# Five phase borders worked off in two halves of the tokens

## The chip, the cores and the metric

The kernel runs on one core of a Trainium2 chip. The metric is the device time of one execution in microseconds (us), as the median of the timed runs. TensorE does the matmuls (its weight loads are recorded apart), VectorE and ScalarE the elementwise work, GpSimd splits the weights, and SyncE issues the large transfers.

## The reference, cut to what matters

512 tokens of 1024 features go through three transformer layers: one with an HGRN2 and stick-breaking mixer, one with an mLSTM mixer (both with a gated feed-forward of 2816 features behind a short convolution), and one with dilated and sparse attention and a gated feed-forward. Each layer twice does the same around its mixer or feed-forward:

```python
h = rmsnorm(x, g) * (1.0 + scale) + shift     # scale, shift, gate: from c, one value per feature
x = x + gate * (inner(h) @ w_out)             # the next norm needs all 1024 features of x
```

Between the second and the third layer `x` is normed once more with `final_g`, so that border needs two means in a row. All is float32.

## The kernel before, in words

Activations lie transposed: 8 tiles of 128 features by 512 tokens (`X`). Every float32 product is three fp32r matmuls over high and low parts (`three`, L442): weights high by data high, weights high by data low, weights low by data high. Each has 128 x 128 weights and 512 moving columns, and loads its weights anew.

The weights come as one stream of 302 chunks of 128 x 1024. SyncE loads them into two raw slots, GpSimd splits each into `w_hi` and `w_lo` (`split_at`, L417) in one of four slots (`SPL`), and TensorE raises `pe_done` after each chunk. GpSimd may split chunk n once `pe_done` shows chunk n-4 used, and it first does a one-column operation (`pool_gate`).

The borders are these: even_out to ffn0, down0 to odd_in, odd_out to ffn1, down1 to idx_in (the one with two means), attn_out to ffn2. Called 1 to 5 below. An out phase has 8 chunks, one for each output tile (`tile_chunk`, 24 matmuls); a down phase has 24 chunks, three for each output tile (8, 8 and 6 blocks, 66 matmuls). Output tiles land in the PSUM banks `G[0..3]` in turn.

At a border the engines do this. VectorE adds the gated output tile to `X` (`residual`, L1032), ScalarE squares the tile into one of two slots (`square`, L1636), VectorE adds the square to `sq_acc` (L1299), for the last tile not. TensorE sums `sq_acc` and the last square over the features with one-column float32 matmuls (`norm_scale`, L536), with some idle-filling matmuls (`keep_warm`) between. ScalarE takes the root, VectorE the reciprocal, TensorE spreads it over the partitions (`bcast`, L558). Then, for each of 8 tiles: VectorE multiplies by gain and row factor (`scaled`, L1087, one input from PSUM) into one of four `work` slots, ScalarE adds the shift and rounds to `h_hi` (L1651), VectorE takes the rest as `h_lo` (`low`, L1091, from `work` and `h_hi`, both in SBUF). `scaled` runs two tiles ahead of `low`. TensorE starts the next phase with `first_tiles` (L475), which goes through the 8 tiles once and does each for two chunks, so that it uses a tile as soon as it is there. The order on each engine is written out by hand; each engine works its queue in order and waits on counting semaphores.

Of the kernel before, what the change touches and what calls it, by code (L numbers as in the profile page):

```python
# [26 lines left out]
F32 = mybir.dt.float32  # L27
# [6 lines left out]
P = 128  # L34
# [42 lines left out]
WARM = (2, 4, 4, 14)  # L77

# [88 lines left out]
def build(nc, x_in, wstream, adastream, c_in, cols_in, const_in, mask_in, gatew_in, wiw_in, wuk_in, wuv_in, out):  # L167
    with ExitStack() as ctx:
# [155 lines left out]
        rstd_bc = sem("rstd_bcast")  # L324
        t_ready = sem("t_tiles")
# [115 lines left out]
        def _(pe):  # L441
            def three(out_ap, w_h, w_l, r_h, r_l, first, last):  # L442
                pe.matmul(out_ap, w_h, r_h, start=first, stop=False)  # L443
                pe.matmul(out_ap, w_h, r_l, start=False, stop=False)  # L444
                return pe.matmul(out_ap, w_l, r_h, start=False, stop=last)  # L445
# [46 lines left out]
            def tiles(phase, bodies, done=0, wide=2):  # L492
                if done == 0 and phase in FILL:

                    first_tiles(phase, FILL[phase], wide)
# [10 lines left out]
            def down(phase, p_fill):  # L506
                with pe.Fori(0, 2) as i:
                    c = 0
                    for m in range(4):
                        k = 0  # L510
                        pe.wait_ge(gfree[m], i + G0[phase][m])
                        for nk in DOWN:
                            pe.wait_ge(w_split, 12 * i + N0[phase] + c + 1)
                            for kk in range(nk):
                                if m == 0:
                                    pe.wait_ge(p_ready, FT * p_fill + k + 1)
                                s = (N0[phase] + c) % SPL
                                mm = three(G[m][:], whi[s][:, kk * P:(kk + 1) * P], wlo[s][:, kk * P:(kk + 1) * P],
                                           Phi[:, k, :], Plo[:, k, :], k == 0, k == FT - 1)
                                k += 1  # L520
                            mm.then_inc(pe_done, 1)
                            c += 1
# [6 lines left out]
            def partial_sums(c0, tile, first, last):  # L529

                for j in range(NTB):
# [3 lines left out]

            def norm_scale(r):  # L536

                pe.wait_ge(sq_added, KT * r + KT - 1)
                partial_sums(0, sqacc, True, False)
# [3 lines left out]
                if r == 4:  # L543
                    pe.wait_ge(gsq_added, KT)
                    partial_sums(4, work[:, 2, :], False, False)
                    pe.wait_ge(gsq_ready, KT)
                    mm = partial_sums(4, work[:, 1, :], False, True)
                mm.then_inc(norm_sum, 1)
                keep_warm(3 if r == 4 else 1)
# [14 lines left out]
            def norm(r):  # L564
                norm_scale(r)
                bc[0] += 1
                bcast(rstdps, bc[0])
                if r not in (0, 6):
                    keep_warm(WARM[2])

# [178 lines left out]
            tiles("even_out", 2)  # L749
            norm(1)  # L750
            tiles("ffn0", 11)
            down("down0", 0)
            norm(2)

            tiles("odd_in", 2)
# [108 lines left out]
            for u in range(4):  # L864
                tile_chunk(4 + N0["odd_out"] + u, (N0["odd_out"] + u) % SPL, u, 1 + G0["odd_out"][u])
            norm(3)
            tiles("ffn1", 11)
            down("down1", 1)

            norm_scale(4)  # L870
            bc[0] += 1
            bcast(rstdps, bc[0] + 1, 8)
            keep_warm(WARM[2])

            first_tiles("idx_in", FILL["idx_in"])

            bc[0] += 1
# [124 lines left out]
            tiles("attn_out", 2)  # L1002
            norm(5)
            tiles("ffn2", 11)
            down("down2", 2)
# [4 lines left out]
        def _(dve):  # L1010
# [36 lines left out]

            def inverse_rms(n, src):
# [16 lines left out]
            def norm(r, fill, g, shift_scale, first_gain=None):  # L1065

                rms_n[0] += 1
                a = acol[:, 8 * r:8 * r + 8]
# [3 lines left out]
                if first_gain is None:  # L1072
                    ready(inverse_rms(4, rms_n[0]))
                else:
                    ready(inverse_rms(4, rms_n[0]))
                    dve.wait_ge(rstd_ready, inverses_done[0])

                    rms_n[0] += 1
                    link(dve.tensor_tensor(a, a, first_gain, ALU.mult))
                    link(dve.tensor_tensor(rst[:, 4:8], rst[:, 0:4], rst[:, 0:4], ALU.mult))  # L1080
                    dve.tensor_tensor(rst[:, 4:8], rst[:, 4:8], normps[:, 4:8], ALU.mult).then_inc(sig("second_mean"), 1)
                    dve.wait_ge(rms_ready, rms_n[0])
                    link(dve.reciprocal(rst[:, 8:12], rms[:, 8:12]))
                    ready(dve.tensor_tensor(rst[:, 8:12], rst[:, 8:12], rst[:, 0:4], ALU.mult))
                spread()

                def scaled(k):  # L1087
                    dve.scalar_tensor_tensor(out=work[:, k % 4, :], in0=X[:, k, :], scalar=a[:, k:k + 1], in1=rstdps[:],
                                             op0=ALU.mult, op1=ALU.mult).then_inc(t_ready, 1)

                def low(k):  # L1091

                    dve.wait_ge(hhi_ready, KT * fill + k + 1)
                    b = shift_scale[0] + k
                    dve.scalar_tensor_tensor(out=Hlo[:, k, :], in0=work[:, k % 4, :], scalar=modv[:, b:b + 1],
                                             in1=Hhi[:, k, :].bitcast(F32), op0=ALU.add, op1=ALU.subtract).then_inc(h_ready, 1)
# [194 lines left out]
            def residual_tiles(phase, r, gate):  # L1291

                dve.wait_ge(mod_added, gate // 4 - 1)
                for m in range(KT):
                    residual(N0[phase] + m, m, m % 4, gate)
                    if m < KT - 1:
                        add_square_prev(r, m)

            def add_square_prev(r, m):  # L1299
                dve.wait_ge(sq_ready, KT * r + m + 1)  # L1300
                dve.wait_ge(sq_added, KT * r + m)
# [8 lines left out]
            norm(1, 2, col("norm_ffn_g", 0, 8), (24, 32))  # L1310
# [31 lines left out]
            def down(phase, r, gate, group=None, turn=0, gain=False):  # L1342
# [4 lines left out]
                for i in range(2):  # L1347
                    for m in range(4):
                        residual(12 * i + N0[phase] + 3 * m + 2, 4 * i + m, m, gate)
# [12 lines left out]
            norm(2, 3, col("norm_mix_g", 8, 8), (48, 56))  # L1362
# [138 lines left out]
            norm(3, 5, col("norm_ffn_g", 8, 8), (72, 80))  # L1501
            ffn("ffn1", 1, COL["fconv_w"] + 66, 25, 21, C2, 11)
            down("down1", 4, 88, gain=True)
            norm(7, 6, col("g_attn", 0, 8), (96, 104), first_gain=col("final_g", 0, 8))
# [119 lines left out]
            norm(6, 8, col("g_ffn", 0, 8), (120, 128))  # L1624
# [6 lines left out]
        def _(act):  # L1631
            link = Link(act, act_step)
            nrm = [0]
            scaled = [0]

# [3 lines left out]
            def norm(r, fill, shift, table=None):  # L1639
                nrm[0] += 1  # L1640
                act.wait_ge(norm_sum, nrm[0])
                act.activation(rms[:, 0:4], normps[:, 0:4], ACT.Sqrt, bias=col("eps"), scale=1.0 / D).then_inc(rms_ready, 1)
                if table is not None:
                    act.preload_act_table(table)
                high_tiles(shift)

            def high_tiles(shift):
                for k in range(KT):

                    act.wait_ge(t_ready, scaled[0] + k + 1)  # L1650
                    act.activation(Hhi[:, k, :], work[:, k % 4, :], ACT.Identity, bias=modv[:, shift + k:shift + k + 1]).then_inc(hhi_ready, 1)  # L1651
                scaled[0] += KT

# [153 lines left out]
            def squares(r, phase, gain=None):  # L1807

                act.preload_act_table(ACT.Sqrt)
                with act.Fori(0, 2) as i:  # L1810
                    for u in range(4):

                        act.wait_ge(gfree[u], i + G0[phase][u] + 1)
                        act.wait_ge(sq_added, 4 * i + KT * r + u - 1)
                        square(4 * i + u, u % 2)
                        if gain is not None:
                            act.wait_ge(gsq_added, 4 * i + u + 1)
                            act.activation(work[:, u % 2, :], X[:, ds(4 * i + u, 1), :].rearrange("p a t -> p (a t)"), ACT.Square,
                                           scale=cols[:, ds(4 * i + gain + u, 1)]).then_inc(gsq_ready, 1)

            squares(1, "even_out")
            norm(1, 2, 24, ACT.Gelu_apprx_tanh)
# [23 lines left out]

            act.wait_ge(pe_done, N0["odd_in"])
# [3 lines left out]
            norm(2, 3, 48, ACT.Silu)  # L1851
# [77 lines left out]
            norm(3, 5, 72, ACT.Gelu_apprx_tanh)  # L1929
# [198 lines left out]
```

## Time and profile before

| | us |
|---|---|
| median of 3 timed runs (lowest, highest) | 2023.68 (2023.48, 2025.96) |
| profiled execution, whole | 2021.82 |
| profiled execution, span from first to last instruction | 2020.0 |
| TensorE busy | 1947.8 (96%) |
| GpSimd busy | 1183.6 (59%) |
| VectorE busy | 1048.7 (52%) |
| ScalarE busy | 447.2 (22%) |

Times within the execution are counted from its first instruction. A busy engine is one with an instruction on record; a matmul's record is longer than the step from one matmul to the next, since they are pipelined. float32 matmuls (not fp32r) leave two records each. The mean granted TensorE clock was 0.983 of full.

### The profile page before, as it was taken

The page shows a single profiled execution, that of the slowest core. Times are in us where ns is not written, and L with a number is a line of the kernel's source. Part 1 is how long each engine was busy: PE and PEld are TensorE (multiplying, and loading weights), DVE is VectorE, ACT ScalarE, POOL GpSimd, SP SyncE. Part 2 cuts the span into 40 slices and gives each one's busy share as a digit, 9 for nine tenths or more (in the row PEclk, how much of TensorE's full clock was granted, in tenths as well). Part 3 has the DMA queues.
Part 4 walks back from the last instruction along what each step waited for, and adds up shares of the span by engine and source line. Part 5 has one row for each costly group of instructions (what it writes and reads, how often), then busy time and mean ns, then how long its engine had stood idle before and what let it go on. Part 6 is the DMA issues. An engine that isn't in the chain of part 4 may idle for free.

```text
span 2020.0 us, 25249 instructions
## 1 busy us (share of the span) xinstructions
PE 1947.8 (96%) x8772; PEld 1563.7 (77%) x8772; DVE 1048.7 (52%) x1588; ACT 447.2 (22%) x762; POOL 1183.6 (59%) x907
## 2 busy tenths in 40 slices
PE   7999999999999999998999999999997899999998
PEld 6787868888888877655888888886775588888886
DVE  5566257766646353557666663234857563232222
ACT  3302342112110022432221111012116421111100
POOL 3653325878877956223688787743550157666673
PEclk7999999999999999998999999999999999999999
DMA  7432223555555422111355553321210023232232
GB/s 298 167 125 73 94 94 104 188 187 203 188 200 179 156 91 83 42 42 46 133 201 193 194 188 127 104 95 63 84 63 22 11 84 104 93 101 97 95 113 73
DMA packets 67518, 242.25 MB, mean 120 GB/s; under 512 B 7642, under 2 KB 8026, under 8 KB 67458
## 3 DMA queue, kind: packets, MB, share of 16 engines
q1 hardware_dynamic: 65536, 237.01, 34.2%
q10 hardware_dynamic: 1922, 4.40, 0.6%
q8 instruction: 42, 0.69, 0.1%
q14 instruction: 18, 0.15, 0.0%
HBM read 239.28 MB, written 2.10 MB: 119 GB/s over the span
## 4 chain that ended last, share of the span: by engine, by line
PE 89%; DVE 4%; ACT 3%; issue 2%; DMA 1%; POOL 1%; SPq 0%; DVEq 0%; ACTq 0%; POOLq 0%
PE gemm L443 24%; PE gemm L445 23%; PE gemm L444 23%; PE gemm L470 2%; PE gemm L472 2%; PE gemm L471 2%; DMA w_raw<-wstream 1%; PE mix L646 1%; PE mix L443 1%; PE gemm L799 1%; PE mix L444 1%; PE mix L445 1%; PE mix L952 1%; PE gemm L813 1%; PE mix L554 1%
## 5 line engine op out<-in xcount | busy, mean ns | idle before, releaser
L427 POOL TENSOR_TENSOR w_lo<-w_raw,w_hi 128x1024 fp32r<-128x1024 f32 x302 | 741.1, 2454 | 25.2
L443 PE MATMUL gemm<-h_hi,w_hi 128*128 128x512 f32 x1616 | 635.4, 393 | 14.3 <-DVE h_lo L1123 6.4
L444 PE MATMUL gemm<-h_lo,w_hi 128*128 128x512 f32 x1616 | 631.1, 391 | 0.0
L445 PE MATMUL gemm<-h_hi,w_lo 128*128 128x512 f32 x1616 | 631.0, 390 | 0.0
L424 POOL TENSOR_TENSOR pool_gate<-pool_gate 128x1 f32<-128x1 f32 x298 | 104.2, 350 | 764.6 <-PE gemm L445 619.7
L443 PEld LDWEIGHTS gemm<-h_hi,w_hi 128*128 128x128 f32 x1616 | 305.0, 189 | 83.9 <-issue 13.4
L425 POOL TENSOR_SCALAR w_hi<-w_raw 128x1024 fp32r<-128x1024 f32 x302 | 351.1, 1163 | 18.4 <-DMA w_raw<-wstream 18.4
L445 PEld LDWEIGHTS gemm<-h_hi,w_lo 128*128 128x128 f32 x1616 | 304.7, 189 | 64.0
L444 PEld LDWEIGHTS gemm<-h_lo,w_hi 128*128 128x128 f32 x1616 | 305.2, 189 | 62.7
L1017 DVE CUSTOM_DVE_ANT_0 ada_raw<-ada_raw,c_act 128x1024 f32<-128x1024 f32 x128 | 219.4, 1730 | 106.2 <-DMA ada_raw<-adastream 106.2
L445 PE MATMUL gemm<-p_hi,w_lo 128*128 128x512 f32 x528 | 205.4, 389 | 0.0
L443 PE MATMUL gemm<-p_hi,w_hi 128*128 128x512 f32 x528 | 205.4, 389 | 0.0
L444 PE MATMUL gemm<-p_lo,w_hi 128*128 128x512 f32 x528 | 205.4, 389 | 0.0
L1035 DVE SCALAR_TENSOR_TENSOR x_res<-gemm,modv,x_res 128x512 f32<-128x512 f32 x48 | 35.9, 749 | 245.6 <-PE gemm L445 245.6
L1330 DVE TENSOR_TENSOR work<-work,gemm 128x512 f32<-128x512 f32 x66 | 45.4, 688 | 176.4 <-PE gemm L445 138.6
L1637 ACT ACTIVATE sq_tile<-x_res 128x512 f32 (+1 forms) x56 | 35.3, 631 | 448.5 <-DVE x_res L1035 435.4
L1332 DVE TENSOR_TENSOR p_lo<-work,p_hi 128x512 f32 x66 | 95.0, 1440 | 61.4 <-ACT p_hi L1842 61.4
L1302 DVE TENSOR_TENSOR sq_acc<-sq_acc,sq_tile 128x512 f32<-128x512 f32 x42 | 95.8, 2282 | 37.1 <-ACT sq_tile L1637 37.1
L443 PEld LDWEIGHTS gemm<-p_hi,w_hi 128*128 128x128 f32 x528 | 99.1, 188 | 20.7
L445 PEld LDWEIGHTS gemm<-p_hi,w_lo 128*128 128x128 f32 x528 | 99.1, 188 | 20.5
L444 PEld LDWEIGHTS gemm<-p_lo,w_hi 128*128 128x128 f32 x528 | 99.1, 188 | 20.5
L1836 ACT ACTIVATE work<-work 128x512 f32<-128x512 f32 x44 | 27.8, 633 | 308.8 <-DVE work L1325 308.8
(323 smaller groups left out, 1999.9 us busy)
## 6 DMA issues: line engine op xcount, KB each, us to landing
w_raw<-wstream SPq DMA_DIRECT2D x302, 512.0 KB, 3.5
ada_raw<-adastream SPq DMA_DIRECT2D x128, 512.0 KB, 4.3
a_early<-adastream SPq DMA_DIRECT2D x8, 1024.0 KB, 13.2
out<-x_res SPq DMA_DIRECT2D x8, 256.0 KB, 2.2
x_res<-x_in SPq DMA_DIRECT2D x2, 512.0 KB, 6.4
c_act<-c_in ACTq DMA_DIRECT2D x2, 512.0 KB, 7.2
x_res<-x_in ACTq DMA_DIRECT2D x2, 512.0 KB, 9.0
b_dist<-const_in ACTq DMA_DIRECT2D x1, 512.0 KB
```

The costliest lines, as they stand in the source:

```text
L424: pool.tensor_tensor(pgate[:], pgate[:], pgate[:], ALU.mult)
L425: pool.tensor_scalar(whi[s][:], raw[:, u % RAW, :], 1.0, 0.0, ALU.mult, ALU.add).then_inc(w_hi_done, 1)
L427: pool.tensor_tensor(wlo[s][:], raw[:, u % RAW, :], whi[s][:].bitcast(F32), ALU.subtract).then_inc(w_split, 1)
L443: pe.matmul(out_ap, w_h, r_h, start=first, stop=False)
L444: pe.matmul(out_ap, w_h, r_l, start=False, stop=False)
L445: return pe.matmul(out_ap, w_l, r_h, start=False, stop=last)
L470: pe.matmul(G[j][:], a, wh, start=(k == 0), stop=False)
L471: pe.matmul(G[j][:], a, wl, start=False, stop=False)
L1017: dve.tensor_tensor_reduce(w, w, c, 1.0, start, ALU.mult, ALU.add, total).then_inc(ada_used, 1)
L1302: dve.tensor_tensor(sqacc[:], sqacc[:], sqt[:, m % 2, :], ALU.add).then_inc(sq_added, 1)
L1330: dve.tensor_tensor(work[:, 2 + jj, :], y, G[2 * jj + 1][:], ALU.mult).then_inc(gfree[2 * jj + 1], 1)
L1332: dve.tensor_tensor(Plo[:, ds(2 * i + jj, 1), :].rearrange("p a t -> p (a t)"), work[:, 2 + jj, :], Phi[:, ds(2 * i + jj, 1), :].rearrange ...
```

## The change

At each of the five borders, the last output tile is computed for tokens 0 to 255 first and for tokens 256 to 511 after, the first half into `G[3]`, the second into `M[1]`, with the same weights loaded again. The sums, roots, row factors, `scaled`, `h_hi` and `h_lo` are done for each half on its own, with 256 columns; the sums and row factors of the first half stand among TensorE's matmuls of the second half of the last tile (`BACK` says before which block), and those of the second half among the first-half matmuls of the next phase's first two chunks (`FRONT`). The next phase's first two chunks are done for all 8 tiles of the first half and then for all 8 of the second. `PLACES` says behind which `low` VectorE puts the second half's residual and reciprocal, and where ScalarE puts square, root and the load of the next function table. The chunk counter `pe_done` of the last output tile rises in its second half only.

At odd borders the square of tile 6 is no longer added to `sq_acc` by VectorE but summed by TensorE (`ADDS`). The `keep_warm` matmuls at the five borders are gone. ScalarE's small loads for odd_in and idx_in are issued after the last `h_hi`, not before the norm. The `Fori` loops of the down phases and of `squares` are unrolled.

```diff
+HALVES = (slice(0, 256), slice(256, 512))
+ADDS = {1: 6, 2: 7, 3: 6, 4: 7, 5: 6, 6: 7}
+BACK = {1: (0, 1, 3), 2: (0, 1, 5), 3: (0, 1, 3), 4: (0, 1, 9), 5: (0, 1, 3)}
+FRONT = {1: (2, 5), 2: (2, 4), 3: (2, 5), 4: (3, 7), 5: (2, 5)}
+PLACES = {1: (1, 4), 2: (7, 7), 3: (1, 4), 4: (4, 7), 5: (1, 4)}
...
+            def first_halves(phase, r):
+                late, spread = FRONT[r]
...
+                for half, cols in enumerate(HALVES):
+                    for k in range(KT):
+                        if half == 0 and k == late:
+                            last_sums(r, 1)
+                        if half == 0 and k == spread:
+                            half_rows(r, 1)
+                        if half == 0:
+                            pe.wait_ge(h_half, KT * (r - 1) + k + 1)
+                        else:
+                            pe.wait_ge(h_ready, KT * FILL[phase] + k + 1)
+                        for u in range(2):
+                            if half == 0 and k == 0 and u == 0:
+                                pe.wait_ge(w_split, N0[phase] + 2)
+                            s = (N0[phase] + u) % SPL
+                            mm = three(G[u][:, cols], whi[s][:, k * P:(k + 1) * P], wlo[s][:, k * P:(k + 1) * P],
+                                       Hhi[:, k, cols], Hlo[:, k, cols], half == 0 and k == 0, k == KT - 1, True)
+                            if half == 1 and k == KT - 1:
+                                mm.then_inc(pe_done, 1)
+
+            def last_halves(n, counts, hi, lo, uses, r):
+                early, late, spread = BACK[r]
+                pe.wait_ge(gfree[3], uses)
+                for half, cols in enumerate(HALVES):
+                    out_ap = (G[3], M[1])[half][:, cols]
+                    k = 0
+                    for c, nk in enumerate(counts):
+                        s = (n + c) % SPL
+                        if half == 0:
+                            pe.wait_ge(w_split, n + c + 1)
+                        for kk in range(nk):
+                            if half == 1 and k == early:
+                                first_sums(r)
+                            if half == 1 and k == late:
+                                last_sums(r, 0)
+                            if half == 1 and k == spread:
+                                half_rows(r, 0)
+                            mm = three(out_ap, whi[s][:, kk * P:(kk + 1) * P], wlo[s][:, kk * P:(kk + 1) * P],
+                                       hi[:, k, cols], lo[:, k, cols], k == 0, k == sum(counts) - 1)
+                            k += 1
+                        if half == 1:
+                            mm.then_inc(pe_done, 1)
+                    if half == 0:
+                        mm.then_inc(half_done, 1)
...
@@ VectorE, norm
+                after_residual, after_inverse = PLACES[r]
+                residual_half(last, gate, r, 0)
+                inverse(0)
                 scaled(0)
                 scaled(1)
-                for k in range(KT):
-                    low(k)
-                    if k + 2 < KT:
-                        scaled(k + 2)
+                n = 2
+                for t in range(2 * KT):
+                    low(t)
+                    if t == after_residual:
+                        residual_half(last, gate, r, 1)
+                    if t == after_inverse:
+                        inverse(1)
+                    while n < 2 * KT and n <= t + 2 and (n < KT or t >= after_inverse):
+                        scaled(n)
+                        n += 1
...
@@ ScalarE, norm
+                square_half(r, 0, gain)
+                roots_of(r, 0)
+                for t in range(2 * KT):
...
+                    act.activation(Hhi[:, k, cols], work[:, k % 4, cols], ACT.Identity,
+                                   bias=modv[:, shift + k:shift + k + 1]).then_inc(hhi_ready if half else hhi_half, 1)
+                    if t == min(after_residual + 1, after_inverse):
+                        square_half(r, 1, gain)
+                    if t == after_inverse:
+                        roots_of(r, 1)
+                        if table is not None:
+                            act.preload_act_table(table)
```

## Rows read from the trace of the kernel before

**Rows 1.** Page, parts 1 and 4: busy shares; the last chain's share by engine.
```profile
PE 1947.8 (96%) x8772; PEld 1563.7 (77%) x8772; DVE 1048.7 (52%) x1588; ACT 447.2 (22%) x762; POOL 1183.6 (59%) x907
...
PE 89%; DVE 4%; ACT 3%; issue 2%; DMA 1%; POOL 1%; SPq 0%; DVEq 0%; ACTq 0%; POOLq 0%
```
**Rows 2.** Chain of waits at border 1: start us, us, engine and tile.
```profile
337.79 0.79 PE mix L532 x8
...
343.89 0.76 DVE h_lo L1095
...
344.90 0.47 PE gemm L443
```
**Rows 3.** TensorE's timeline at border 4: start us, us, line, operation.
```profile
1339.96 0.95 PE L532 MATMUL mix<-cst,sq_acc 128*128 128x1 f32 x8
...
1351.21 0.47 PE L443 MATMUL gemm<-h_hi,w_hi 128*128 128x512 f32 x1 [0.86 <-DVE h_lo L1095]
```
**Rows 4.** Timeline of all engines at border 1.
```profile
332.86 0.39 PE L443 MATMUL gemm<-h_hi,w_hi 128*128 128x512 f32 x1
332.86 0.19 PEld L444 LDWEIGHTS gemm<-h_lo,w_hi 128*128 128x128 f32 x1
...
337.39 0.40 PE L445 MATMUL gemm<-h_hi,w_lo 128*128 128x512 f32 x1
...
337.63 0.95 PE L532 MATMUL mix<-cst,sq_acc 128*128 128x1 f32 x8
337.83 0.75 DVE L1035 SCALAR_TENSOR_TENSOR x_res<-gemm,modv,x_res 128x512 f32<-128x512 f32 x1 [1.17 <-PE gemm L445]
...
338.09 1.05 POOL L425 TENSOR_SCALAR w_hi<-w_raw 128x1024 fp32r<-128x1024 f32 x1
...
338.50 0.65 DVE L1070 SCALAR_TENSOR_TENSOR acol<-modv,cols 128x8 f32<-128x8 f32 x1
...
339.22 2.35 POOL L427 TENSOR_TENSOR w_lo<-w_raw,w_hi 128x1024 fp32r<-128x1024 f32 x1
...
340.84 1.28 ACT L1644 ACT_TABLE_LOAD   x1
...
342.35 1.41 DVE L1088 SCALAR_TENSOR_TENSOR work<-x_res,acol,mix 128x512 f32<-128x512 f32 x2 [1.25 <-PE mix L554]
```
**Rows 5.** TensorE's timeline: eight transposes in a row.
```profile
1547.61 1.09 PE L971 MATMUL gemm<-cst,ada_raw 128*128 128x128 f32 x8
```
**Rows 6.** Timeline of weight loads: sixteen for one-column matmuls in a row.
```profile
1342.68 1.87 PEld L532 LDWEIGHTS mix<-cst,work 128*128 128x128 f32 x16
```
**Rows 7.** Groups by form (busy us, mean ns | idle); one line's runs (min/median/max ns).
```profile
L1526 DVE SCALAR_TENSOR_TENSOR b_score<-ada_raw,b_wi,b_score 128x256 f32<-128x256 f32 x7 | 3.3, 477 | 0.0
...
L1095 DVE SCALAR_TENSOR_TENSOR h_lo<-work,modv,h_hi x40: 744/746/753, 343.9 to 1656.0; 128x512 fp32r<-128x512 f32 x40
```
**Rows 8.** GpSimd's busy time while ffn0's first two chunks run.
```profile
345.00:355.90 10.90, 0.43 (x2) 1.00 0.07 26
```
**Rows 9.** Timeline of VectorE and GpSimd in the attention stage.
```profile
1474.54 1.23 POOL L425 TENSOR_SCALAR w_hi<-w_raw 128x1024 fp32r<-128x1024 f32 x1
1474.89 4.21 DVE L1567 SCALAR_TENSOR_TENSOR b_bias<-b_dist 128x512 f32<-128x512 f32 x2
1475.85 2.70 POOL L427 TENSOR_TENSOR w_lo<-w_raw,w_hi 128x1024 fp32r<-128x1024 f32 x1
```
**Rows 10.** All runs of two VectorE lines: min/median/max ns, first and last start.
```profile
L1567 DVE SCALAR_TENSOR_TENSOR b_bias<-b_dist x8: 677/684/2874, 1474.9 to 1528.5; 128x512 f32<-128x512 f32 x8
L1302 DVE TENSOR_TENSOR sq_acc<-sq_acc,sq_tile x42: 693/2588/2727, 306.2 to 1994.2; 128x512 f32<-128x512 f32 x42
```
**Rows 11.** Stretches: length, busy PE, PEld, DVE, ACT, POOL, then granted clock.
```profile
1345.00:1347.00 2.00, 2.00 (x7) 1.38 (x6) 1.00 (x6) 0.30 (x1) 0.00 (x0) 0.51 0.95 327
1484.00:1487.00 3.00, 1.01 (x5) 0.50 (x3) 0.00 (x0) 1.96 (x4) 1.83 (x3) 1.00 0.53 173
1487.00:1492.00 5.00, 4.75 (x19) 3.80 (x20) 1.23 (x7) 1.39 (x2) 1.72 (x1) 0.66 0.30 106
```

More of the change, by code:

```diff
@@ L493, in tiles, with out_tiles @@
+            def out_tiles(phase, r):
+                for u in range(3):
+                    tile_chunk(4 + N0[phase] + u, (N0[phase] + u) % SPL, u, 1 + G0[phase][u])
+                last_halves(N0[phase] + 7, (KT,), Hhi, Hlo, 1 + G0[phase][3], r)
+            def tiles(phase, bodies, done=0, wide=2, halves=None):
                 if done == 0 and phase in FILL:
-                    first_tiles(phase, FILL[phase], wide)
+                    if halves:
+                        first_halves(phase, halves)
+                    else:
+                        first_tiles(phase, FILL[phase], wide)
@@ L748, in _ @@
             pe.wait_ge(h_ready, KT * FILL["even_out"] + 7)
[L749 to L755, printed above, removed]
+            tiles("even_out", 1)
+            out_tiles("even_out", 1)
+            tiles("ffn0", 11, halves=1)
+            down("down0", 0, 2)
+            tiles("odd_in", 2, halves=2)
             pe.wait_ge(sig("gw_split"), 1)
@@ L863, in _ @@
                 tile_chunk(N0["odd_out"] + u, (N0["odd_out"] + u) % SPL, u, G0["odd_out"][u])
[L864 to L877, printed above, removed]
+            out_tiles("odd_out", 3)
+            tiles("ffn1", 11, halves=3)
+            down("down1", 1, 4)
+            first_halves("idx_in", 4)
             bcast(M[1], bc[0])
@@ L1001, in _ @@
                 values(p)
[L1002 to L1005, printed above, removed]
+            tiles("attn_out", 1)
+            out_tiles("attn_out", 5)
+            tiles("ffn2", 11, halves=5)
+            down("down2", 2, 6)
             norm(6)
@@ L1063, in _, with norm @@
             rms_n = [0]
[L1065 to L1068 removed]
+            def norm(r, slot, fill, g, shift_scale, last, gate, first_gain=None):
+                a = acol[:, 8 * slot:8 * slot + 8]
                 dve.wait_ge(mod_added, shift_scale[1] // 4 - 1)
@@ L1085, in norm @@
[L1085 to L1093, printed above, removed]
-                    b = shift_scale[0] + k
-                    dve.scalar_tensor_tensor(out=Hlo[:, k, :], in0=work[:, k % 4, :], scalar=modv[:, b:b + 1],
-                                             in1=Hhi[:, k, :].bitcast(F32), op0=ALU.add, op1=ALU.subtract).then_inc(h_ready, 1)
+                    ready(dve.reciprocal(rst[:, c], rms[:, c]))
@@ L1647, in high_tiles, with roots_of @@
[L1647 to L1651, printed above, removed]
-                scaled[0] += KT
+                c = slice(2 * half, 2 * half + 2)
+                act.activation(rms[:, c], normps[:, c], ACT.Sqrt, bias=col("eps"), scale=1.0 / D).then_inc(rms_ready, 1)
+            def roots_of(r, half):
+                root(half)
+                if r == 4:
+                    act.wait_ge(sig("second_mean"), half + 1)
+                    act.activation(rms[:, 8 + 2 * half:10 + 2 * half], rst[:, 4 + 2 * half:6 + 2 * half], ACT.Sqrt, bias=col("eps"),
+                                   scale=1.0 / D).then_inc(rms_ready, 1)
@@ L1809, in squares @@
                 act.preload_act_table(ACT.Sqrt)
[L1810 to L1819, printed above, removed]
+                last_use[0] = G0[phase][3] + 2
+                for m in range(KT if r not in PLACES else KT - 1):
+                    act.wait_ge(gfree[m % 4], m // 4 + G0[phase][m % 4] + 1)
+                    act.wait_ge(sq_added, ADDED[r] + m)
+                    square(m, m % 2)
+                    if gain is not None:
+                        act.wait_ge(gsq_added, m + 1)
+                        act.activation(work[:, m % 2, :], X[:, m, :], ACT.Square, scale=gain[:, m:m + 1]).then_inc(gsq_ready, 1)
             squares(1, "even_out")
-            norm(1, 2, 24, ACT.Gelu_apprx_tanh)
+            norm(1, 24, None, ACT.Gelu_apprx_tanh)
             def ffn(phase, f, taps, bias):
```

217 lines of the change are left out of this document (148 added, 69 removed).

## The prediction

> **What bounds the kernel now.** First I read the page's shares: TensorE is busy 96% of the span and 89% of the chain that ended last runs over it [rows 1]. Other engines count only where TensorE waits. The chain of waits at one border shows such a place: after the last out matmul it goes from the norm's one-column sums through the rest of the norm to the first h_lo, and only then to the first matmul of the next phase [rows 2]. The same chain stands at five borders; the fourth, with a second mean, is longer [rows 3].
>
> The timeline gives the step of a full matmul: 21 of them from 332.86 to 337.39, so 4.53/20 = 0.2265 us [rows 4]. Its record is 0.39 to 0.40 long, so a record outlasts the streaming by 0.163, and the last out matmul streams until 337.63, where the sums begin [rows 4]. The first of the next phase streams from about 344.98 (its record ends at 345.37; 345.37 - 0.163 - 0.2265) [rows 2]. So a normal border costs 7.35 us. The fourth costs 11.33 by the same reckoning, from 1339.96 to 1351.29 [rows 3].
>
> I count each border from the start of its last out chunk to the end of the next phase's first two chunks (48 matmuls, 10.87 us). Before, with 24 matmuls in a last chunk (borders 1, 3, 5): 5.44 + 7.35 + 10.87 = 23.66. With 66 (border 2): 14.95 + 7.35 + 10.87 = 33.17. Border 4: 14.95 + 11.33 + 10.87 = 37.15.
>
> **TensorE's own work after.** Each of those matmuls becomes two of 256 columns: 144 at an odd border, 228 at an even one, 888 in all. No row shows such a matmul. Half of 0.2265 is 0.1133. An instruction pair that loads 128 columns of weights steps by (1.09 - 0.28)/7 = 0.116 in the transposes [rows 5]. If the excess of 0.2265 over 512 columns at 2.4 GHz (0.2133) is a fixed price, the step is 0.1067 + 0.013 = 0.120. I take 0.12; the bounds are 0.113 and, if the load hid nothing, 0.189 + 0.107 = 0.30, from the load's record [rows 4]. That upper end is far from the transposes' 0.116, where load and matmul already overlap. The norm's f32 passes stay and step by about 0.112 (16 loads in 1.87 us: 1.87 less the last one's 0.19, over 15) [rows 6]: 32 passes at odd borders, 24 at border 2, 40 at border 4. The keep-warm matmuls go. So with no wait at all an odd border takes 144 x 0.12 + 32 x 0.112 = 20.9, border 2 30.1, border 4 31.8.
>
> The row on loads: the next load is issued beside the running matmul (start 332.86 for both) and the step stays 0.2265, although load and stream together would be about 0.32 [rows 4]. The Trainium skill, page "TensorE: Matmul & The Clock Gate", section "Part 3: Packing small matmuls", says a weight load overlaps a running matmul only where the row groups differ. By it 888 matmuls would step by some 0.21 instead of 0.12 and the change would lose about 80 us more; this trace, with full-height loads, disagrees.
>
> **VectorE, with nothing in its way.** A border now needs 16 scaled and 16 h_lo operations of 256 columns. The nearest row (same instruction and two SBUF inputs, 256 columns) is 0.477, against h_lo's 0.746 for 512 [rows 7]. Two scaled tiles in a row take 1.41, so they step by 0.66, 0.083 less than the record [rows 4]; half ones then step by 0.394, a half tile costs VectorE 0.79 against TensorE's 0.72. At an odd border (0 is the start of the last chunk): first half ends at 2.88; half residual 3.08 to 3.56; square to 4.0, hidden by the sums over sq_acc; last sums 5.03; root, reciprocal, rows 6.39; scaled 7.03; h_lo 0 at 8.09, ready when TensorE is through the second half at 8.64. That is the gain: the 7.35 is gone. But 16 half tiles from there, plus the second residual and reciprocal and the 1.28 us table load [rows 4], which now sits between h_hi 4 and 5, put h_lo 15 at 21.3 and TensorE's end at 22.7. Gain 1.0 each, VectorE-bound. Border 2: its first half tiles hide beneath 66 matmuls; end 30.6, gain 2.6. Border 4: 33.4, gain 3.8. Sum 3 x 1.0 + 2.6 + 3.8 = 9.4 us faster.
>
> **VectorE beside GpSimd.** This decides my sign. h_lo reads two SBUF tiles (work and h_hi). All its 40 runs took 0.744 to 0.753 [rows 7], but in none of them did GpSimd split: its two operations in the gap end at 341.57 [rows 4], and in the 10.9 us of the first two chunks it is busy 0.43 [rows 8], since all four weight slots are full. Other VectorE instructions of two SBUF inputs did meet GpSimd's splitting. A scalar_tensor_tensor of 0.684 took 2.874 at its longest [rows 10]: two in a row took 4.21, the first held until w_hi ended, the second, which found w_lo just started, until w_lo ended; and that w_lo took 2.70 for 2.40, as it had waited for the first [rows 9]. The eight-column gain at 338.50 ended with w_hi after 0.65 [rows 4], and the squares' adds have a median of 2.588 against a minimum of 0.693 [rows 10]. Residual and scaled, with one input in PSUM, keep 0.75 beside GpSimd [rows 4].
> The Trainium skill, page "SBUF — State Buffer", section "Who interferes with whom", says that a VectorE instruction with two SBUF inputs contends with a GpSimd one that reads SBUF, for the whole instruction. By h_lo's own rows the sum would stay at 9.4 faster; by the rule, which the rows of other lines bear out, it turns.
>
> After the change they meet. A chunk is split as soon as TensorE frees its slot: w_hi begins 0.46 us after the last matmul (337.63 to 338.09), w_lo ends at 341.57, and the next gate follows [rows 4]; some 3.6 us a chunk. At an odd border the last chunk's slot comes free at 8.64, so w_hi and w_lo fall on h_lo 2 and 3: w_lo holds h_lo 3 from 10.75 to 12.82. Some of that hides the table load. End 23.7: gain 0.
> At border 2 the three last chunks (8, 8, 6) are needed by both halves, and their slots come free only in the second, at 12.6, 15.5 and 17.6. GpSimd then splits three chunks in a row, 13.1 to 25, each stretched to 3.95 by two h_lo that slip in between its operations. Only those two get through per chunk: h_lo 7 starts at 25.0 instead of 18.3. The new order puts the second residual behind h_lo 7, and TensorE stands in its queue, before tile 2 of the next phase, at the wait for that half's squares: from 19.1 to 26.5, with tiles 2 to 7 and all later matmuls behind it. Then come the sums, rows and 14 tiles: 26.5 + 0.9 + 14 x 0.72 = 37.4. Loss 4.3. Border 4, residual after h_lo 4: the same meeting gives 38.9, loss 1.75. Sum 3 x 0 + 4.3 + 1.75 = 6.0 us slower.
>
> The clock: it read 1.00 while TensorE worked; in 1345 to 1347, after it had done only one-column sums and short keep-warm work, it read 0.51, and 0.66 after a stretch with 1.0 us of work in 3 [rows 11]. An idle of 7.4 us at border 2 should do the same: some 3.4 us at 1.2 GHz lose 1.7, all on the path; border 4 hides most, 0.5. Sum 8.2.
>
> The rest at nothing. The small loads of odd_in and idx_in are issued after the last h_hi instead of before the norm: 1.3 and 1.8 us on ScalarE's queue, then VectorE's splits; TensorE has two chunks (10.9 us) before it needs a freed bank. If that cover fails, about 2 us. Unrolled loops and static addresses: within 1 us either way.
>
> **Forecast.** The profiled execution took 2021.82 (span 2020.0 and 1.8 around it) and lies 1.9 below the median of the timed runs, 2023.68. 2021.8 + 8.2 = 2030.0; as a median 2031.9.
>
> **Rivals.**
> - Other side, faster: the meetings don't happen or don't hold h_lo. Speaking for it: no h_lo row shows one. Against it: rows of the same instruction form. The modelled nine meetings with a w_lo (one at each odd border, three at each even one) cost 9.4 + 6.0 = 15.4, 1.7 each; the sign turns where five or fewer of them fall on the path. 2023.7 - 9.4 = 2014.3.
> - Milder: they meet, but the third chunk's w_raw is late, its split falls into the gap of sums and root, and the clock stays up. Border 2 then loses about 1.5, border 4 nothing, odd ones gain 0.3: 2024.5.
> - Half matmuls far dearer, 0.19 (the load's record as the step): 888 x 0.07 = 62 more, partly under VectorE's pace: about 2085.
>
> **Chances.** Forecast 0.50 (own range 2026 to 2040: steps of 0.113 to 0.13 give -2.8 to -10.8 before the clock), faster rival 0.24, milder 0.22, dear matmuls 0.04. The range 2014 to 2040 leaves out the last and the edges. 0.2% is 4 us, what this kernel's measurement can tell from no change. Slower: 0.44 + 0.07 + 0.04 = 0.55; same: 0.05 + 0.14 + 0.02 = 0.21; faster 0.24.
>
> **What would show it.** h_lo of 256 columns with a median near 0.48 but a maximum near 2.6, and GpSimd busy beside it at borders 2 and 4. TensorE idle some 7 us before tile 2 of odd_in, waiting for the square. The half matmuls' step: 0.12. Odd borders ending within 1 us of 23.7. Wrong if h_lo's maximum stays below 0.6, or if the split of the held chunks falls elsewhere.

## The result, and the profile after

The changed kernel takes 2037.01 us (median of 4, 2036.82 to 2037.63) against 2023.58 for the kernel before (4 runs, 2023.15 to 2025.96): ratio 1.0067, 95% interval 1.0055 to 1.0080. It is 13.4 us slower, where 8.2 was forecast. The profiled executions differ by 15.2 us of span (2035.2 against 2020.0); the mean granted clock fell from 0.983 to 0.977.

The lengths of the five borders, in us, each from the first matmul of the last out chunk to the end of the next phase's first two chunks (border 4: to the spreading of row factors that stands right behind those two chunks), read from TensorE's timeline. The forecast counted from 23.66, 33.17 and 37.15; the timeline of the kernel before gives 0.04 to 0.08 more:

| border | before | forecast | after |
|---|---|---|---|
| 1 | 23.72 | 23.7 | 24.46 |
| 2 | 33.25 | 39.1 (37.4 and 1.7 of clock) | 39.55 |
| 3 | 23.70 | 23.7 | 24.57 |
| 4 | 37.22 | 39.4 (38.9 and 0.5) | 41.69 |
| 5 | 23.71 | 23.7 | 23.16 |

Their sum is 11.8 us more than before, 6.3 of it at border 2 and 4.5 at border 4. The other 3.4 lie outside the borders: 2.2 before border 1, where the code is unchanged, and 1.1 between borders 4 and 5. More on them below.

The page's parts 1 and 4 answer to [rows 1]: TensorE is as busy as before, and VectorE's share of the last chain is up from 4% to 6%.

```profile
PE 1951.1 (96%) x9166; PEld 1588.3 (78%) x9166; DVE 1077.2 (53%) x1679; ACT 460.7 (23%) x814; POOL 1188.1 (58%) x907
...
PE 87%; DVE 6%; ACT 2%; issue 2%; DMA 1%; POOL 1%; SPq 0%; DVEq 0%; ACTq 0%; POOLq 0%
```

TensorE's timeline after shows the step of half a matmul: 24 of them start between 334.43 and 337.18, 2.75/23 = 0.12 us, the forecast value, against 0.2265 for a whole one [rows 4].

```profile
334.43 0.28 PE L462 MATMUL gemm<-h_hi,w_hi 128*128 128x256 f32 x1
...
337.18 0.28 PE L464 MATMUL gemm<-h_hi,w_lo 128*128 128x256 f32 x1
```

The query of h_lo's line (min/median/max in ns) answers to the last of [rows 7]. The median is what a free half tile takes; the maximum is that of a held one, as in [rows 10]:

```profile
L1217 DVE SCALAR_TENSOR_TENSOR h_lo<-work,modv,h_hi x80: 472/480/2229, 342.3 to 1673.1; 128x256 fp32r<-128x256 f32 x80
```

VectorE's timeline at border 2, and then GpSimd's over the same microseconds. Each h_lo that starts beside a w_hi or a w_lo ends just after it (705.76 + 1.03 = 706.79 on a w_hi that ends at 706.52; 707.11 + 2.23 = 709.34 on a w_lo that ends at 709.06). The scaled tiles, with one input in PSUM, stay at 0.47 in the same stretch. Two h_lo get through per chunk, as forecast (the row of 2.56 holds two, 2.17 and 0.47):

```profile
705.76 1.03 DVE L1217 SCALAR_TENSOR_TENSOR h_lo<-work,modv,h_hi 128x256 fp32r<-128x256 f32 x1
706.72 0.47 DVE L1205 SCALAR_TENSOR_TENSOR work<-x_res,acol,mix 128x256 f32<-128x256 f32 x1
707.11 2.23 DVE L1217 SCALAR_TENSOR_TENSOR h_lo<-work,modv,h_hi 128x256 fp32r<-128x256 f32 x1
...
710.99 2.19 DVE L1217 SCALAR_TENSOR_TENSOR h_lo<-work,modv,h_hi 128x256 fp32r<-128x256 f32 x1
...
714.82 2.56 DVE L1217 SCALAR_TENSOR_TENSOR h_lo<-work,modv,h_hi 128x256 fp32r<-128x256 f32 x2
717.31 0.47 DVE L1156 SCALAR_TENSOR_TENSOR x_res<-mix,modv,x_res 128x256 f32<-128x256 f32 x1
```
```profile
705.47 1.05 POOL L444 TENSOR_SCALAR w_hi<-w_raw 128x1024 fp32r<-128x1024 f32 x1
706.61 2.45 POOL L446 TENSOR_TENSOR w_lo<-w_raw,w_hi 128x1024 fp32r<-128x1024 f32 x1
709.02 0.37 POOL L443 TENSOR_TENSOR pool_gate<-pool_gate 128x1 f32<-128x1 f32 x1
709.36 1.05 POOL L444 TENSOR_SCALAR w_hi<-w_raw 128x1024 fp32r<-128x1024 f32 x1
710.49 2.41 POOL L446 TENSOR_TENSOR w_lo<-w_raw,w_hi 128x1024 fp32r<-128x1024 f32 x1
```

TensorE's timeline there: it stands 6.9 us before tile 2, waiting for the second half's square, and then steps at 0.21 instead of 0.12:

```profile
711.14 0.28 PE L464 MATMUL gemm<-h_hi,w_lo 128*128 128x256 f32 x1
718.28 1.01 PE L616 MATMUL mix<-cst,sq_tile 128*128 128x1 f32 x4 [6.86 <-ACT sq_tile L1818]
719.16 0.56 PE L462 MATMUL gemm<-h_hi,w_hi 128*128 128x256 f32 x1
...
720.37 0.41 PE L464 MATMUL gemm<-h_hi,w_lo 128*128 128x256 f32 x1
720.58 0.41 PE L462 MATMUL gemm<-h_hi,w_hi 128*128 128x256 f32 x1
```

At border 1 the same happens on a small scale: h_lo 3 is held by the one w_lo that it meets, and TensorE waits 1.5 us for it (both timelines):

```profile
345.23 2.19 DVE L1217 SCALAR_TENSOR_TENSOR h_lo<-work,modv,h_hi 128x256 fp32r<-128x256 f32 x1
...
347.47 0.39 PE L462 MATMUL gemm<-h_hi,w_hi 128*128 128x256 f32 x1 [1.52 <-DVE h_lo L1217]
```

Stretches of all five borders (length; busy PE, PEld, DVE, ACT, POOL; granted clock). At borders 1, 2 and 4 a stall of TensorE is followed by a lower clock, and at 2 and 4 VectorE then idles while it waits for TensorE's sums and rows. Borders 3 and 5 have a stall of 1.5 and 1.4 us too, up to 991.76 and 1664.23, and the clock behind it is 1.00 (the stretches from 991.8 and from 1664.2). At border 3 it was low earlier, in the last out chunk, where TensorE didn't stand (982 to 986):

```profile
347.00:352.00 5.00, 4.53 (x25) 4.53 (x26) 3.93 (x11) 2.33 (x5) 0.13 (x1) 0.66 0.59 211
...
711.40:718.30 6.90, 0.04 (x2) 0.02 (x1) 6.38 (x7) 1.64 (x4) 5.22 (x4) 0.88 0.43 123
718.30:724.00 5.70, 5.70 (x29) 5.70 (x30) 1.04 (x3) 2.07 (x4) 0.00 (x0) 0.55 0.22 83
...
982.00:986.00 4.00, 4.00 (x24) 4.00 (x24) 0.79 (x3) 0.37 (x2) 0.00 (x0) 0.61 0.75 262
991.80:997.00 5.20, 5.20 (x43) 5.18 (x44) 5.20 (x15) 3.14 (x7) 0.00 (x0) 1.00 0.61 205
...
1357.80:1361.50 3.70, 0.04 (x1) 0.00 (x0) 3.70 (x6) 0.96 (x3) 2.45 (x2) 1.00 0.46 134
1361.50:1368.50 7.00, 6.99 (x33) 6.99 (x34) 2.45 (x9) 1.78 (x5) 0.00 (x0) 0.52 0.22 74
...
1664.20:1668.00 3.80, 3.77 (x31) 3.76 (x32) 3.80 (x11) 2.23 (x5) 0.00 (x0) 1.00 0.37 138
```

### The profile page after: what moved, and what is told of

It reads as the page before. It is cut to its first block, busy times and chain, and to the rows that moved or that the text cites. A ratio compares the mean times of both kernels' runs of the same rounds, so it can differ in the third digit from the quotient of the medians.

```text
span 2035.2 us, 25972 instructions
## 1 busy us (share of the span) xinstructions
PE 1951.1 (96%) x9166; PEld 1588.3 (78%) x9166; DVE 1077.2 (53%) x1679; ACT 460.7 (23%) x814; POOL 1188.1 (58%) x907
## 4 chain that ended last, share of the span: by engine, by line
PE 87%; DVE 6%; ACT 2%; issue 2%; DMA 1%; POOL 1%; SPq 0%; DVEq 0%; ACTq 0%; POOLq 0%
PE gemm L462 23%; PE gemm L463 23%; PE gemm L464 23%; PE gemm L489 2%; PE gemm L491 2%; PE gemm L490 2%; DVE h_lo L1217 1%; DMA w_raw<-wstream 1%; PE mix L759 1%; PE mix L462 1%; PE mix L463 1%; PE mix L464 1%; PE gemm L924 1%; PE gemm L910 1%; PE mix L1053 1%
## 5 line engine op out<-in xcount | busy, mean ns | idle before, releaser
L462 PE MATMUL gemm<-h_hi,w_hi 128*128 128x512 f32 (+1 forms) x1696 | 651.1, 384 | 16.3 <-DVE h_lo L1217 6.4
L463 PE MATMUL gemm<-h_lo,w_hi 128*128 128x512 f32 (+1 forms) x1696 | 644.6, 380 | 0.0
L464 PE MATMUL gemm<-h_hi,w_lo 128*128 128x512 f32 (+1 forms) x1696 | 644.3, 380 | 0.0
L462 PEld LDWEIGHTS gemm<-h_hi,w_hi 128*128 128x128 f32 x1696 | 322.4, 190 | 81.9 <-DVE h_lo L1217 7.5
L464 PEld LDWEIGHTS gemm<-h_hi,w_lo 128*128 128x128 f32 x1696 | 322.5, 190 | 59.8
L463 PEld LDWEIGHTS gemm<-h_lo,w_hi 128*128 128x128 f32 x1696 | 322.7, 190 | 58.5
L464 PE MATMUL gemm<-p_hi,w_lo 128*128 128x512 f32 (+1 forms) x528 | 200.7, 380 | 0.0
L463 PE MATMUL gemm<-p_lo,w_hi 128*128 128x512 f32 (+1 forms) x528 | 200.7, 380 | 0.0
L462 PE MATMUL gemm<-p_hi,w_hi 128*128 128x512 f32 (+1 forms) x528 | 200.7, 380 | 0.0
L1771 ACT ACTIVATE sq_tile<-x_res 128x512 f32<-128x512 f32 x51 | 32.1, 631 | 404.9 <-DVE x_res L1136 391.7
```

Of the source, the lines that this page charges most:

```text
L462: pe.matmul(out_ap, w_h, r_h, start=first, stop=False, skip_group_check=part)
L463: pe.matmul(out_ap, w_h, r_l, start=False, stop=False, skip_group_check=part)
L464: return pe.matmul(out_ap, w_l, r_h, start=False, stop=last, skip_group_check=part)
```

## The experiments

Theory A: the loss is h_lo held by GpSimd's splits, the waits behind it, and the clock that falls after them. All times are medians of 5 or more timed runs, and the kernel before ran beside them (2022.5 to 2023.5). Border lengths are from each kernel's profile.

### 1. The meetings taken away: t in PSUM

The scaled tiles go to the idle banks of gemm2 and gemm3, in four slots of 256 columns, so h_lo has one SBUF input.

```diff
+def t_slot(k):
+    return G[2 + k % 2][:, HALVES[k % 4 // 2]]
-...scalar_tensor_tensor(out=work[:, k % 4, cols], in0=X[:, k, cols], ...)
+...scalar_tensor_tensor(out=t_slot(k), in0=X[:, k, cols], ...)
-...scalar_tensor_tensor(out=Hlo[:, k, cols], in0=work[:, k % 4, cols], ...)
+...scalar_tensor_tensor(out=Hlo[:, k, cols], in0=t_slot(k), ...)
-act.activation(Hhi[:, k, cols], work[:, k % 4, cols], ...)
+act.activation(Hhi[:, k, cols], t_slot(k), ...)
```

> Changed kernel with the scaled tiles t of the five half-borders written to the idle PSUM banks of gemm2 and gemm3 instead of SBUF, so h_lo reads one SBUF tile (h_hi) and one PSUM tile. Theory A (the loss is h_lo held by GpSimd's splits, and the waits and clock drops that follow from it): h_lo of 256 columns has a maximum under 0.6 us, the borders measure about 22.7 (odd), 30.6 (border 2) and 33.4 (border 4) us from the first half matmul to the end of the next phase's first two chunks, no 1.2 GHz stretch at borders 2 and 4, and the median is about 2014, 2012 to 2018. Rival B (the loss is TensorE's own work in halves: more instructions, one-column sums between them, a lower granted clock for that mix): the maximum of h_lo falls but the borders stay within 2 us of 24.5, 39.6 and 41.7, median above 2030. Rival C (a new price: ScalarE and VectorE reading PSUM are slower): h_lo or h_hi records grow above 0.6 us and the median lands at 2020 to 2030.

Measured: 2015.23 us, ratio to before 0.9964 (0.9950 to 0.9978). Borders 22.29, 30.60, 22.30, 35.93, 22.30. h_lo's line, then VectorE's and GpSimd's timelines at border 2: the same instruction, beside the same w_hi and w_lo, is not held at all.

```profile
L1220 DVE SCALAR_TENSOR_TENSOR h_lo<-gemm,modv,h_hi x80: 476/479/489, 341.7 to 1647.9; 128x256 fp32r<-128x256 f32 x80
```
```profile
706.16 0.48 DVE L1220 SCALAR_TENSOR_TENSOR h_lo<-gemm,modv,h_hi 128x256 fp32r<-128x256 f32 x1
...
707.57 0.48 DVE L1220 SCALAR_TENSOR_TENSOR h_lo<-gemm,modv,h_hi 128x256 fp32r<-128x256 f32 x1 [0.16 <-ACT h_hi L1803]
```
```profile
706.13 1.06 POOL L447 TENSOR_SCALAR w_hi<-w_raw 128x1024 fp32r<-128x1024 f32 x1
707.27 2.38 POOL L449 TENSOR_TENSOR w_lo<-w_raw,w_hi 128x1024 fp32r<-128x1024 f32 x1
```

Rivals B (TensorE's own work in halves) and C (PSUM dearer) fall as the cause of the loss: the same TensorE work, in the same order, is 21.8 us faster than in the changed kernel, and faster than before. The other two operations on t have hardly changed with its place: the median of scaled is 0.481 us instead of 0.473, that of h_hi 0.474 instead of 0.509. One part of rival B stands, a lower clock in the last chunk of some borders; more on it below. Border 2 is the contention-free model's 30.6 to the digit. Border 4 missed its 33.4, for two reasons that the timeline and the windows show. A two-column product with two SBUF inputs stood for a whole w_lo (which ran from 1343.67 to 1346.08), and the clock was low in the last down chunks:

```profile
1343.76 2.33 DVE L1197 TENSOR_TENSOR rstd<-rstd 128x2 f32<-128x2 f32 x1
```
```profile
1330.00:1334.00 4.00, 4.00 (x23) 4.00 (x23) 0.81 (x5) 0.56 (x2) 0.00 (x0) 0.57 0.02 4
```

### 2 and 3. Borders undone

```diff
+OLD = (2,)          # experiment 3: (1, 3, 5)
+for _r in OLD:      # these borders run the code of the kernel before
+    del PLACES[_r]
+    ADDS[_r] = 7
```

> Changed kernel with border 2 alone done whole (512 columns) as in the kernel before, the other four in halves. Theory A: border 2 goes from 39.55 back to 33.2 us, the others stay: 2037.0 - 6.4 = 2030.6, within 1.5. Rival D (the 3.2 us that the changed kernel loses outside the five borders also belong to border 2, by its later small loads): 2037.0 - 9.6 = 2027.4. Rival E (phase shift decides the clock drops anywhere): other borders change by over 1 us each.

> Changed kernel with the three odd borders (1, 3, 5) done whole as in the kernel before, borders 2 and 4 in halves. Theory A: odd borders were worth +0.8, +0.9 and -0.5 us against before, so undoing them gives 2037.0 - 1.2 = 2035.8, within 1.5. Rival: the odd borders carry the 3.2 us lost elsewhere too, 2032.6. Sum rule: this loss against before plus what border 2 alone gives back must leave about 4.5 for border 4.

Measured: 2032.78 (ratio 1.0042, 1.0026 to 1.0057) and 2035.64 (1.0059, 1.0046 to 1.0072). With border 2 whole the kernel gives back 4.2, not 6.4, a miss, though in the profile that border is down to 33.05: border 4 in the same profile is 43.62 and border 5 24.49, 1.9 and 1.3 longer than in the changed kernel. That is rival E (other borders change) in part. Rival D (more than border 2's own share comes back) is not borne out by the median, but the seven runs lie far apart (2027.83 to 2037.49). With the odd borders whole 1.4 us come back, as expected; yet in its profile borders 2 and 4 are 40.15 and 43.60, 2.5 longer together, so the match is in part luck. A border's price depends on where the clock falls in it, and undoing one does not subtract cleanly.

### 4. The order of VectorE's queue

```diff
-PLACES = {1: (1, 4), 2: (7, 7), 3: (1, 4), 4: (4, 7), 5: (1, 4)}
+PLACES = {1: (1, 4), 2: (3, 5), 3: (1, 4), 4: (2, 5), 5: (1, 4)}
```

> Changed kernel with the second half's residual placed after h_lo 3 at border 2 (instead of 7) and after h_lo 2 at border 4 (instead of 4), its inverse after h_lo 5 at both. GpSimd's splits still hold h_lo. Theory A with the queue order as the second half of the cause: the meetings keep h_lo 7 at the same place, but VectorE no longer stands idle for sums, root and rows (5.1 us at border 2, 4.2 at border 4) and TensorE no longer waits 7 us before tile 2, so the 1.2 GHz stretches at both borders go: border 2 about 34.5, border 4 about 37.5, median 2025 to 2029. Rival F (the meetings alone decide, the order of the queue is hidden): median above 2034.

Measured: 2029.06 (1.0019, 1.0010 to 1.0029), 8 faster than the changed kernel. Border 2 is 32.81, border 4 is 40.19. h_lo's maximum stays 2231 ns. At border 2 the three w_lo still hold an h_lo each (2.23, 1.82 and 2.15 us), but TensorE gets to the second half's sums almost without a wait, where it stood 6.86 us in the changed kernel, and later waits 0.96 at most (VectorE's and TensorE's timelines):

```profile
708.52 0.47 DVE L1156 SCALAR_TENSOR_TENSOR x_res<-mix,modv,x_res 128x256 f32<-128x256 f32 x1
708.92 0.47 DVE L1205 SCALAR_TENSOR_TENSOR work<-x_res,acol,mix 128x256 f32<-128x256 f32 x1
709.30 1.82 DVE L1217 SCALAR_TENSOR_TENSOR h_lo<-work,modv,h_hi 128x256 fp32r<-128x256 f32 x1
```
```profile
709.50 0.61 PE L616 MATMUL mix<-cst,sq_tile 128*128 128x1 f32 x4
...
712.59 0.71 PE L654 MATMUL mix<-cst,rstd 128*128 128x128 f32 x4 [0.96 <-DVE rstd L1190]
```

So border 2, with all its meetings, is shorter than before (33.25): it was the residual's place behind the eighth h_lo that turned the held ones into a long wait of TensorE. Rival F falls. Border 4 gained only 1.5 of the 4.2 expected. Its rows stand before tile 7 in TensorE's queue, so behind h_lo 6, and that now follows the second mean's reciprocals on VectorE; and in its last down chunks TensorE stepped at 0.22 instead of 0.12 for 5 us.

### 5 and 6. The clock

```diff
 for k in range(KT):
+    if half == 0 and k == fill_at:     # 2 at border 2, 3 elsewhere
+        keep_warm(fill_n)              # 26, 15, 6; then 14, 8, 3
```

> Changed kernel plus dependency-free 256-column keep-warm matmuls where TensorE stands: 26 before the second half's sums at border 2, 15 at border 4, 6 before tile 3 at the odd borders. The meetings stay as they are. Theory A (the 1.2 GHz stretches behind the stalls follow from TensorE's idle time and cost part of the loss): the stretches of 3.4 and 6.8 us behind the stalls go, border 2 falls from 39.55 to about 37.5, border 4 from 41.7 to about 40, odd ones from 24.5 to about 23.5; median about 2031, 2029 to 2033. Rival G (the low clock is hidden behind VectorE's pace): median 2036 to 2038, borders unchanged within 0.5.

Measured: 2040.15 (1.0082, 1.0069 to 1.0096), a miss of mine: I had sized a filler at 0.23 us, from rows that group records, but one filler leaves two records (52 for the 26), and the 26 took 11.2 us, 0.43 each. The square was there at 718.76 and the sums started at 722.99, 4.2 us later; border 2 took 41.32. The granted clock behind the fillers was 1.00, so the idea was still open:

> The kernel with fillers again, sized by what one of them took there (26 in 11.2 us, 0.43 each): 14 before the sums at border 2, 8 at border 4, 3 before tile 3 at the odd ones, so that none outlasts the wait it fills. Theory A (the 1.2 GHz stretches cost part of the loss): with the overrun of the earlier run taken off, border 2 is 41.3 - 4.6 = 36.7, border 4 about 38.5, odd ones about 23.3 where the clock had dropped; sum against the changed kernel -8, median 2029, 2027 to 2032. Rival G (the low clock is hidden, the earlier run was slow for more than the overrun): 2035 to 2038, border 2 above 39.

Measured: 2031.32 (1.0048, 1.0034 to 1.0061), 5.7 faster than the changed kernel (4.6 if each is taken against the kernel before that ran beside it, 2022.51 and 2023.58). The 4.6 us of overrun in the expectation were 4.2. Borders 23.31, 37.24, 24.55, 38.62, 23.14. The stretches of border 2 answer to those shown of the changed kernel:

```profile
709.50:716.50 7.00, 6.26 (x30) 5.18 (x29) 6.59 (x7) 1.78 (x4) 5.43 (x4) 1.00 0.41 128
716.50:723.00 6.50, 6.40 (x54) 6.41 (x55) 3.76 (x10) 3.75 (x8) 0.00 (x0) 1.00 0.20 74
```

The meetings are unchanged (h_lo's maximum is 2232 ns), so by these two profiles the low clock behind the stalls cost 2.3 at border 2, 3.1 at border 4 and 1.2 at border 1. Rival G falls. Border 3 kept its 24.55: there the clock falls earlier, in the last out chunk itself, where no filler stands:

```profile
978.00:982.00 4.00, 4.00 (x23) 4.00 (x24) 0.84 (x3) 0.42 (x2) 0.00 (x0) 0.59 0.76 262
```

### 7. How long a hold lasts

```diff
-pool.tensor_tensor(wlo[s][:], raw[...], whi[s][:], ALU.subtract)
+pool.tensor_tensor(wlo[s][:, 0:512], raw[... 0:512], whi[s][:, 0:512], ALU.subtract)
+pool.tensor_tensor(wlo[s][:, 512:1024], raw[... 512:1024], whi[s][:, 512:1024], ALU.subtract)
```

> Changed kernel with GpSimd's w_lo of 1024 columns computed in two instructions of 512. Theory A with the hold lasting for the GpSimd instruction that runs (not for its chunk): h_lo's maximum falls from 2.23 to about 1.2 us, three h_lo instead of two get through per chunk, so a blocked tile takes about 1.45 instead of 1.92 us and the seven of border 2 finish about 3.3 us earlier, border 4 gains about 2, odd ones up to 1: median about 2030, 2027 to 2033. Rival H (the hold is by total traffic, each engine just gets half): h_lo's longest stays near 2.2 and nothing moves, 2036 to 2038.

Measured: 2030.10 (1.0039, 1.0025 to 1.0053), 6.9 faster than the changed kernel; borders 22.88, 36.92, 24.11, 38.52, 24.05. h_lo's maximum fell from 2229 to 1499 ns (1.2 us was expected). At border 2, VectorE's and GpSimd's timelines:

```profile
706.38 1.12 DVE L1218 SCALAR_TENSOR_TENSOR h_lo<-work,modv,h_hi 128x256 fp32r<-128x256 f32 x1
...
707.83 1.12 DVE L1218 SCALAR_TENSOR_TENSOR h_lo<-work,modv,h_hi 128x256 fp32r<-128x256 f32 x1
```
```profile
705.88 1.34 POOL L446 TENSOR_TENSOR w_lo<-w_raw,w_hi 128x512 fp32r<-128x512 f32 x1
707.19 1.48 POOL L447 TENSOR_TENSOR w_lo<-w_raw,w_hi 128x512 fp32r<-128x512 f32 x1
```

A held h_lo ends 0.3 us after the one GpSimd instruction that it met, whatever comes next on GpSimd, so three h_lo get through a chunk instead of two. Rival H falls.

### 8 to 10. The version that beats both, and what it leaves

On top of experiment 1: border 4's products with one operand in PSUM, and its sums moved; then w_lo in pieces too; then, instead of the pieces, the table load behind the last h_hi.

```diff
-link(dve.tensor_tensor(rst[:, c4], rst[:, c], rst[:, c], ALU.mult))
+link(dve.tensor_tensor(normps[:, c8], rst[:, c], normps[:, c4], ALU.mult))
-BACK  4: (0, 1, 9)   FRONT  4: (3, 7)
+BACK  4: (0, 3, 9)   FRONT  4: (2, 7)
```

> Kernel with t in PSUM (2015.2) and, at border 4, the two-column products of the second mean with one operand in PSUM, so none has two SBUF inputs (one of them stood 2.33 us there), the first half's last sums three k steps later and the second half's one step earlier. Theory A: no VectorE instruction of border 4 lasts over 1 us, TensorE's 1.1 us wait before the rows of tile 7 goes, border 4 falls from 35.9 to 33.5 to 35 (the lower end if its 1.2 GHz stretch of 3.4 us goes too): median 2013 to 2015. Rival: the TensorE queue is the bound there by now, no change, 2015.2 within 1.

> The previous kernel with w_lo in two pieces as well. Theory A: h_lo no longer meets GpSimd, and the other VectorE instructions with two SBUF inputs stand beside TensorE's stream, so nothing on the path is held: same as the previous kernel within 1.5 us. Rival: phases outside the borders have held instructions on the path (some stand 2.2 to 2.9 us), and shorter pieces give back 3 us or more.

> Kernel with t in PSUM and border 4 tuned (2014.3), and the table load of the three odd borders issued after the last h_hi instead of between h_hi 4 and 5, where it holds VectorE 0.85 us at each. Theory A (VectorE's pace is what is left at the odd borders): each odd border falls from 22.3 to 21.5, median 2011.8, within 1.5. Rival: the load now stands before the next phase's first ScalarE instruction and delays a freed bank, no change or slower.

Measured: 2014.28 (0.9961, 0.9947 to 0.9975), 2016.43 (0.9968, 0.9958 to 0.9979), 2014.20 (0.9959, 0.9945 to 0.9972). Border 4 went from 35.93 to 33.27, the model's 33.4, yet the median moved by only 0.95, inside its interval. Not all of that is the edit: in experiment 9, with the same code for it, the clock fell in the last down chunks again, as it had in experiment 1, and border 4 took 34.80. So some 1.1 us are the products and sums, and 1.5 the clock. Once h_lo is free, shorter splits bring nothing: 2.2 slower, with intervals that overlap, and 0.6 more than was expected. The later table load shortened border 3 from 22.30 to 21.35, but at borders 1 and 5 the clock fell in the last chunk (22.54, 22.56) and the median did not move (2011.8 was expected): its gain is not shown by the times.

## Why the prediction was right, and what it missed

- **Direction and mechanism: right, and shown.** Moving t to PSUM, which takes h_lo's second SBUF input away, turns 13.4 slower into 8.2 faster. The faster rival (2014.3) had the right price for a world without meetings; it failed on its one premise.
- **Half a matmul, 0.12: right.** The rival with dear matmuls falls with it.
- **VectorE's pace without contention: right.** 30.60 for 30.6 at border 2 (experiment 1), 33.27 for 33.4 at border 4 (8), 22.3 for 22.7 at odd ones (experiment 1).
- **VectorE beside GpSimd: right to 0.4 us.** With the clock held up (6) border 2 is 37.24 for 37.4, border 4 is 38.62 for 38.9, border 1 is 23.31 for 23.7. TensorE stood from 711.4 to 718.3, 19.3 to 26.2 us into the border; the forecast said 19.1 to 26.5. The trace thus agrees with the section "Who interferes with whom" of the Trainium skill's page "SBUF — State Buffer": h_lo is held beside a split (2.23 us) with two SBUF inputs and not with one (0.489 us at most). The longest hold was 2.23, where 2.6 was forecast.
- **The clock: the term that was mis-sized.** The forecast had 1.7 at border 2, 0.5 at border 4 and nothing at odd ones, 2.2 in all. Experiment 6 measures 2.3, 3.1 and 1.2 at borders 2, 4 and 1; border 3 lost about as much (24.57 against 23.2 at border 5, where the clock stayed up). That is some 8, and it leaves about 3.9 of the 11.8 for the meetings, where 6.0 was forecast (the odd borders came out 0.4 to 0.5 shorter each). The two misses go against each other, so the sum is nearer than its terms. Where the clock term went wrong: no row ahead of the result shows the 3.4 us at 1.2 GHz that it counts with; TensorE worked at 0.50 from 718.3 to 723.4 at border 2, 5.1 us, and from 1361.7 to 1368.5 at border 4, 6.8 us. And I called border 4's mostly hidden. It was not: VectorE needs TensorE's sums and rows for the second half, so the low clock sits on the chain there. At border 1 I had left out that h_lo 3, held 2.19 us, makes TensorE wait 1.5 us. The milder rival, in which the clock stays up, falls too.
- **A low clock without a stall: not in the forecast at all.** At border 3 it fell inside the last out chunk, before TensorE had waited. Over the ten profiles with odd borders in halves this is so at 17 of 30, and at none of the six odd borders done whole (kernel before and experiment 3). It costs 1.1 to 1.2 us each (in experiment 8 border 5 is 23.41 with it, and 1 and 3 are 22.3 without; in experiment 10 borders 1 and 5 are 22.5 with it, and 3 is 21.35 without). So this part of the loss goes with TensorE's work in halves and not with h_lo; what makes it come at one border and not at the next is open.
- **Outside the borders: 3.4 us of the profile that the forecast did not have.** Nothing shows that the change owns them. From the end of border 4 to the start of border 5 it is 274.4 us in the changed kernel and 273.3 in the one before, and in the ten experiments, which all run the changed code there, 270.3 to 274.9. Before border 1 the code is the same, yet border 1 starts at 332.2 us in the kernel before, 332.3 in experiment 4, 333.9 in 1, 334.4 in the changed kernel and 336.7 in 2. The clock in 100 to 200 us was 1.00, 1.00, 0.98, 0.98 and 0.95. What sets off that fall in one execution and not in another is open. It is one reason why single profiles of these kernels lie up to 5 us from their medians.
- **Small loads and unrolled loops at nothing:** the stretch from the end of border 2 to the start of border 3 is 245.8 us in both kernels, so no cost shows for odd_in's, and that from border 1 to border 2, with a down phase unrolled, is 333.2 in both; no run tried them alone, and for idx_in's the stretch behind border 4 scatters too much to tell.

## What to carry to other kernels

Before work is moved under a running stream, look at which engine will be running beside it in its new place, and at where its operands are: here the same instruction cost 0.48 or 2.2 us, and the kernel 2015 or 2037, by whether one operand was in SBUF or in an idle PSUM bank. Where a hold can't be avoided, keep instructions that the bound engine waits for (here the second residual) ahead of the held ones. And price a long stall of TensorE at more than its length: here 3.7 and 6.9 us were followed by a low clock, 1.4 to 1.5 us once in three times, and what is done at the low clock may be on another engine's chain.

## What was not expected of the hardware

- The hold goes by the GpSimd instruction that is met, not by the size of the held one: a product of two columns, 0.16 us elsewhere, took 2.33 beside a w_lo of 2.41 (experiment 1).
- A stretch of many one-column and 128-column f32 passes between half matmuls was followed by a clock of 0.57 to 0.61 over 4 us with TensorE busy throughout (1330 to 1334 in experiment 1, 978 to 982 in 6, 982 to 986 in the changed kernel), in some borders and not in others of the same code.
- 256-column f32 keep-warm matmuls cost 0.43 us each, 3.6 times the half matmuls of the gemm (0.12), and held the clock at 1.00 through 7 us in which those had nothing to do.
